# One GpSimd subtraction of 1536 columns instead of three of 512, in a kernel that splits its weights

## The chip, the cores and the metric

The kernel runs on one core of one Trainium2 chip. The metric is the device time of one execution in microseconds (us), the median of several runs. TensorE multiplies matrices, VectorE and GpSimd do element-wise work on SBUF (only VectorE also reads PSUM), ScalarE does activations and copies, and SyncE issues the loads.

## What is computed

One step of a decoder layer over 512 prompt rows and 8 sample rows, 520 tokens in all, with 1024 channels:

```
x <- LN1(alpha*x + 0.5*SwiGLU_1(x))          # first feed-forward part
z  = x @ w_in -> [C | B | h | p | g_a | g_p]
m  = sigmoid(g_a) * (B * conv3(C * h)) + sigmoid(g_p) * pooled(p)
x <- LN2(alpha*x + m @ w_out)
x <- LN3(alpha*x + 0.5*SwiGLU_2(x))          # second feed-forward part

SwiGLU(x) = (silu(x @ wg) * (x @ wu)) @ wd   # wg, wu: 1024 x 2816, wd: 2816 x 1024
```

All is in float32.

## The kernel before

Every operand of TensorE is split in two: a rounded part (hi) and what the rounding leaves, the rest (lo = value - hi). A product is then three passes: hi x hi, hi x lo and lo x hi. For a loaded weight, ScalarE makes hi by a copy to the rounded type, and GpSimd makes lo by a subtraction. TensorE waits for lo by a counter, `lo_ready`.

The tokens are two halves of 260 columns. The 2816 hidden channels of a feed-forward part are 22 columns f of 128. Columns 0 and 1 are made with plain products (the opening). For each of the columns 2 to 21 ("pairs": gate and up together) the kernel uses seven products of half size in place of eight, a Strassen-like scheme. It needs three loaded quarters of the weights, B11, B21 and B22, each 128 partitions x 512 columns, and four sums, T1 to T4. Of these, `weight_sums` (VectorE, L931, L936, L941) makes the sums, with the loaded B12 as one more input; ScalarE rounds; VectorE makes the rests of the sums in `rest_thirteen` (L945) and `rest_twenty_four` (L950); GpSimd makes the rests of B11, B21 and B22 in `split_pair` (L559). B11, B21 and B22 of a pair lie side by side in the three tensors raw, wh and wl.

The columns come in two stretches: 2 to 11, then eight down products; 12 to 21, then eight down products. All orders are written out by hand, one list of instructions for each engine.

TensorE, for pair f: P1 (weight B11), Q5 (T1), Q4 of the pair before (T4), P6 (T2), P2 (B21), Q3 (B22), P7 (T3). In the first pair of a stretch P2 comes right behind P1, and there is no Q4. Each product is 12 matmuls of 260 columns. P1, P2 and Q3 wait for `lo_ready`. Q5 and P7 use T1 and T3 from L945, P6 and Q4 use T2 and T4 from L950. Q4 of pair f also waits for `up_second` of pair f (VectorE, L998), which reads the bank that Q4 writes to.

VectorE, in the body of pair f: up_second(f-1) L998, gated_first(f-1) L1002, the weight sums of f+1 (L931, L936, L941), hid_pair(f-1) L1006 and L1011, rest_thirteen(f+1) L945, hid_rest(f-1) L982, rest_twenty_four(f+1) L950, for f from 3 to 10 the scaling of one tile of the residual (L1076), gate_first(f) L988, up_first(f) L993. L941 waits until the Q4 of two pairs earlier has used the place of T4.

ScalarE, in pair f: copies of three products out of PSUM, the rounding of the three loaded quarters of f+1 in one instruction of 1536 columns, sigmoids, and the roundings of the sums.

GpSimd, for each pair: it waits for the rounding (`hi_ready`) and for the last weight sum of the same pair (`t4_made`), then makes the three rests. Between the stretches, and in the other parts of the layer, it makes the rest of each chunk of weights in one instruction of up to 1536 columns (`split`, L550). It issues no loads.

SyncE loads each quarter as soon as the product that used its place two pairs earlier is done.

Of the kernel before, what the change touches and what calls it, by code (L numbers as in the profile page):

```python
# [30 lines left out]
ALU = mybir.AluOpType  # L31
ACT = mybir.ActivationFunctionType
AX_X = mybir.AxisListType.X
F32 = mybir.dt.float32
# [21 lines left out]
def build(nc, x_prompt, x_sample, state_conv, state_pool, ln1_g, ln1_b, ffn1_wg, ffn1_wu, ffn1_wd,  # L56
# [36 lines left out]
    with ExitStack() as ctx:  # L93
# [3 lines left out]
        def sem(name):  # L97
            return ctx.enter_context(nc.semaphore(name))
# [38 lines left out]
        wh_slot = wh[:].rearrange("p (s k) n -> p s (k n)", k=HK)  # L137
        wl_slot = wl[:].rearrange("p (s k) n -> p s (k n)", k=HK)
        raw_slot = raw[:].rearrange("p (s k) n -> p s (k n)", k=HK)
# [56 lines left out]
        def pair_tiles(ap, kk, h):  # L196

            return ap[:, 2 * kk:2 * kk + 2, h * H:(h + 1) * H]
# [24 lines left out]
        lo_ready = sem("lo_ready")  # L223
# [117 lines left out]
        area, slot, lands, free, landed, hi_no, lo_no = {}, {}, {}, {}, {}, {}, {}  # L341
        free_from = [0] * SLOTS
        landings = [0] * (SLOTS + 5)
        halves = [0, 0]

        def place(what, at, size, product, loaded=True):
            area[what], slot[what] = RING, at
            free[what] = max(free_from[at:at + size])
            free_from[at:at + size] = [number[product]] * size
            if loaded:  # L350
                landing(what, at)
# [21 lines left out]
        def set_of(f):  # L373
            return (f + 1) % 2

        def pair_place(n, f):
            for name, at in SET[set_of(f)].items():
                place((n, name, f), at, 1, (n, FOR[name], f), name[0] == "B")
            halves[0] += 1
            hi_no[n, f] = halves[0]  # L380
            for name in ("B11", "B21", "B22"):
                halves[1] += 1
                lo_no[n, name, f] = halves[1]

        for n in range(2):
            for j in range(4):
                open_place((n, "open", j), j, (FIRST, SECOND)[n], 0)
            for g, (f0, f1) in enumerate(SPANS):
                for f in range(f0, f1):
                    pair_place(n, f)  # L390
                for d in range(K):
                    chunk_place((n, "down", g, d), (8, 11, 0, 3)[d % 4], 3)
                    if (n, g) == (0, 1) and d in (3, 4, 5):
                        for j in {3: (0, 1), 4: (2,), 5: (3,)}[d]:
                            open_place(("mix", j), j, MIXED, number[0, "P7", KF - 1])
            if n == 0:
                for c in range(4, 12 * G):
                    chunk_place(("mix", c), 2 * ((c + 4) % 7), 2)
                for d in range(K - 1):
                    chunk_place(("out", d), 2 * ((12 * G + d + 4) % 7), 2)  # L400
                open_place(("out", K - 1), 0, LAST, number[0, "down", 1, K - 1])
# [6 lines left out]
        def held(part, what):  # L408
            return area[what][part][:, slot[what] * HK:slot[what] * HK + size_of(what), :]
# [15 lines left out]
        def pair_no(n, f):  # L425
            return (KF - 2) * n + f - 1
# [108 lines left out]
        @block.gpsimd  # L535
        def _(pool):
            made = Signal(const_ready)
            made.on(nc.gpsimd.memset(ident[:], 0.0))
            pool.wait_ge(const_ready, 1)
            made.on(nc.gpsimd.affine_select(out=ident[:], in_=ident[:], compare_op=ALU.not_equal, fill=1.0,  # L540
                                            base=0, pattern=[[-1, P]], channel_multiplier=1))
            made.on(nc.gpsimd.memset(ones_mean[:], 1.0 / D))
            assert made.n == 3
            for i in range(max(POOL_WINDOWS) - 1):
                made.on(nc.gpsimd.memset(rcount[:, i:i + 1], 1.0 / (i + 1)))

            def split(what):

                pool.wait_ge(hi_ready, hi_no[what])
                nc.gpsimd.tensor_tensor(held(LO, what), held(RAW, what), held(HI, what).bitcast(F32),  # L550
                                        ALU.subtract).then_inc(lo_ready, 1)

            def split_pair(n, f):
                pool.wait_ge(hi_ready, hi_no[n, f])

                pool.wait_ge(t4_made, pair_no(n, f))
                for name in ("B11", "B21", "B22"):
                    s = slot[n, name, f]
                    nc.gpsimd.tensor_tensor(wl_slot[:, s, :], raw_slot[:, s, :], wh_slot[:, s, :].bitcast(F32),  # L559
                                            ALU.subtract).then_inc(lo_ready, 1)  # L560

            def split_ffn(n, f_first):
                for g, (f0, f1) in enumerate(SPANS):
                    for f in range(f0 if g else f_first, f1):
                        split_pair(n, f)
                    for d in range(K):
                        split((n, "down", g, d))
                        if (n, g) == (0, 1) and d in (3, 4, 5):
                            for j in {3: (0, 1), 4: (2,), 5: (3,)}[d]:
                                split(("mix", j))  # L570

            def x_lo(n, h):

                for kk in range(K // 2):
                    pool.wait_ge(norm[n].round, 4 * h + kk + 1)
                    nc.gpsimd.tensor_tensor(pair_tiles(xl, kk, h), pair_tiles(x32, kk, h),
                                            pair_tiles(xh, kk, h).bitcast(F32), ALU.subtract).then_inc(norm[n].ready, 1)

            for j in range(4):
                split((0, "open", j))  # L580
            split_ffn(0, 2)
            for h in range(2):
                x_lo(0, h)

            nc.gpsimd.memset(pext[:, 0:16], 0.0).then_inc(pads_made, 1)
            nc.gpsimd.memset(uext[:, 0:2], 0.0).then_inc(pads_made, 1)
            for c in range(4, 12 * G):
                split(("mix", c))
            for d in range(K):
                split(("out", d))  # L590
            for j in range(4):
                split((1, "open", j))
            split_pair(1, 2)
            for h in range(2):
                x_lo(1, h)
            split_ffn(1, 3)

            pool.wait_ge(norm[2].offset, 2)
            for kk in range(1, K // 2):
                nc.gpsimd.tensor_tensor(pair_tiles(x32, kk, 1), pair_tiles(x32, kk, 1), offset_twice,  # L600
                                        ALU.subtract).then_inc(pool_minus, 1)
# [1131 lines left out]
```

## Time and profile before

| | before |
|---|---|
| median of 3 runs | 1096.61 us (1094.86 to 1097.17) |
| the profiled execution | 1095.99 us |
| its span, first to last instruction | 1094.2 us |
| TensorE matmul busy | 1059.0 us, 97% |
| VectorE busy | 709.8 us, 65% |
| ScalarE busy | 437.1 us, 40% |
| GpSimd busy | 510.5 us, 47% |
| mean granted TensorE clock | 0.993 |
| L559, the changed line | 120 instructions, 221.7 us |

Busy shares are means over parts of the kernel with different limits. In timelines each row has start and duration in us. An instruction that is shown as running may in part be held up by something that it shares with another engine; the record has no mark for that. Neighbouring records of one engine overlap by a little. In a merged row, xN stands for N instructions of a kind, one behind the other.

### The profile page before, as it was taken

What the parts mean: (1) busy time and instruction counts of PE and PEld (TensorE: products, weight loads), DVE (VectorE), ACT (ScalarE), POOL (GpSimd) and SP (SyncE); (2) the same over time, 40 slices, a digit from 0 to 9 for tenths busy, and PEclk for the clock granted to TensorE, in tenths of its full rate; (3) what the DMA queues carried; (4) which work ended last, traced back from release to release, by engine and by line L of the source; (5) the groups of instructions that cost most, each with busy time, mean ns of one, the idle gap of its engine ahead of it and who ended that gap; (6) DMA issues with size and microseconds to landing.
All of it is one profiled execution on the core that took longest, in us unless ns stands there. A gap on an engine that the chain in (4) does not pass through costs nothing.

```text
span 1094.2 us, 20812 instructions
## 1 busy us (share of the span) xinstructions
PE 1059.0 (97%) x8731; PEld 1050.6 (96%) x8731; DVE 709.8 (65%) x1019; ACT 437.1 (40%) x658; POOL 510.5 (47%) x259
## 2 busy tenths in 40 slices
PE   8999999999999987999999999989999999999996
PEld 7999999999999987999999999988999999999996
DVE  6999921288847866353636437989996116887476
ACT  4555532155553442232231323455554223555224
POOL 4355554154566345444453445334655433566321
PEclk9999999999999998999999999999999999999999
DMA  9133234233355042232332425103334323333402
GB/s 254 36 101 113 73 106 116 77 101 113 97 136 135 18 104 58 83 100 80 97 101 79 115 82 154 40 1 97 97 97 135 88 68 97 114 100 87 120 26 78
DMA packets 195001, 103.29 MB, mean 94 GB/s; under 512 B 4420, under 2 KB 193428, under 8 KB 194901
## 3 DMA queue, kind: packets, MB, share of 16 engines
q1 hardware_dynamic: 194827, 101.85, 32.7%
q8 instruction: 69, 1.13, 0.4%
q10 hardware_dynamic: 82, 0.12, 0.1%
q14 instruction: 23, 0.19, 0.1%
HBM read 99.74 MB, written 2.48 MB: 93 GB/s over the span
## 4 chain that ended last, share of the span: by engine, by line
PE 82%; DVE 11%; issue 3%; ACT 2%; DMA 1%; POOL 1%; SPq 0%; DVEq 0%; ACTq 0%; POOLq 0%
PE ps L1293 13%; PE ps L1295 13%; PE ps L1294 13%; PE ps L1313 13%; PE ps L1310 13%; PE ps L1311 13%; DVE x L1169 1%; DVE xl L915 1%; DVE x L1150 1%; DVE form_lo L966 1%; DMA mixed_raw<-in_w_in_dram 1%; DMA raw<-in_ffn_wd_dram 1%; ACT wh L605 1%; PE ps L1416 1%; PE ps L1356 1%
## 5 line engine op out<-in xcount | busy, mean ns | idle before, releaser
L550 POOL TENSOR_TENSOR wl<-raw,wh 128x1024 fp32r<-128x1024 f32 (+3 forms) x83 | 225.3, 2721 | 237.5 <-ACT wh L605 237.4
L559 POOL TENSOR_TENSOR wl<-raw,wh 128x512 fp32r<-128x512 f32 x120 | 221.7, 1875 | 227.9 <-DVE raw L941 182.6
L605 ACT ACTIVATE wh<-raw 128x1024 fp32r<-128x1024 f32 (+3 forms) x203 | 238.4, 1179 | 193.2 <-DMA raw<-in_ffn_wd_dram 102.8
L1293 PE MATMUL ps<-form_hi,wh 128*128 128x260 f32 x640 | 181.7, 284 | 3.5 <-ACT temps L605 3.5
L1295 PE MATMUL ps<-form_hi,wl 128*128 128x260 f32 x640 | 181.0, 283 | 0.0
L1294 PE MATMUL ps<-form_lo,wh 128*128 128x260 f32 x640 | 180.9, 283 | 0.0
L1310 PE MATMUL ps<-xh,wh 128*128 128x260 f32 x640 | 168.2, 284 | 5.7 <-DVE ymix L1243 5.7
L1311 PE MATMUL ps<-xl,wh 128*128 128x260 f32 x640 | 167.5, 283 | 0.0
L1310 PE MATMUL ps<-hid_hi,wh 128*128 128x260 f32 x544 | 141.9, 282 | 0.0
L1311 PE MATMUL ps<-hid_lo,wh 128*128 128x260 f32 x544 | 141.8, 282 | 0.0
L1293 PE MATMUL ps<-xh,wh 128*128 128x260 f32 x480 | 136.9, 285 | 2.8 <-DVE temps L973 1.5
L1294 PE MATMUL ps<-xl,wh 128*128 128x260 f32 x480 | 136.0, 283 | 0.0
L1295 PE MATMUL ps<-xh,wl 128*128 128x260 f32 x480 | 135.5, 282 | 0.0
L1313 PE MATMUL ps<-xh,wl 128*128 128x260 f32 x640 | 129.5, 284 | 0.0
L1310 PEld LDWEIGHTS ps<-xh,wh 128*128 128x128 f32 x640 | 121.8, 190 | 6.0 <-DVE ymix L1243 6.0
L1293 PEld LDWEIGHTS ps<-form_hi,wh 128*128 128x128 f32 x640 | 120.4, 188 | 4.6 <-issue 3.3
L1311 PEld LDWEIGHTS ps<-xl,wh 128*128 128x128 f32 x640 | 121.3, 190 | 0.0
L1295 PEld LDWEIGHTS ps<-form_hi,wl 128*128 128x128 f32 x640 | 120.6, 188 | 0.0
L1294 PEld LDWEIGHTS ps<-form_lo,wh 128*128 128x128 f32 x640 | 120.5, 188 | 0.0
L1313 PE MATMUL ps<-hid_hi,wl 128*128 128x260 f32 x544 | 109.5, 283 | 0.0
L1310 PEld LDWEIGHTS ps<-hid_hi,wh 128*128 128x128 f32 x544 | 102.5, 188 | 0.0
L1311 PEld LDWEIGHTS ps<-hid_lo,wh 128*128 128x128 f32 x544 | 102.4, 188 | 0.0
(221 smaller groups left out, 2214.4 us busy)
## 6 DMA issues: line engine op xcount, KB each, us to landing
raw<-in_ffn_wg_dram SPq DMA_DIRECT2D x80, 256.0 KB, 3.3
raw<-in_w_in_dram SPq DMA_DIRECT2D x40, 512.0 KB, 3.9
raw<-in_ffn_wd_dram SPq DMA_DIRECT2D x16, 768.0 KB, 5.9
b<-in_ffn_wu_dram SPq DMA_DIRECT2D x40, 256.0 KB, 3.4
raw<-in_ffn_wu_dram SPq DMA_DIRECT2D x40, 256.0 KB, 3.0
raw<-in_ffn_wd_dram SPq DMA_DIRECT2D x16, 640.0 KB, 5.4
raw<-in_w_out_dram SPq DMA_DIRECT2D x7, 512.0 KB, 3.9
xrow<-in_x_prompt_dram SPq DMA_DIRECT2D x4, 512.0 KB, 5.4
```

Of the source, the lines that this page charges most:

```text
L550: nc.gpsimd.tensor_tensor(held(LO, what), held(RAW, what), held(HI, what).bitcast(F32), ALU.subtract).then_inc(lo_ready, 1)
L559: nc.gpsimd.tensor_tensor(wl_slot[:, s, :], raw_slot[:, s, :], wh_slot[:, s, :].bitcast(F32), ALU.subtract).then_inc(lo_ready, 1)
L605: return nc.scalar.activation(out, in_, ACT.Copy)
L915: tt(xl[:, k, :], x32[:, k, :], xh[:, k, :].bitcast(F32), ALU.subtract).then_inc(x_ready, 1)
L966: tt(form_lo[:, i, :], form32[:, i, :], form_hi[:, i, :].bitcast(F32), ALU.subtract).then_inc(form_ready, 1)
L1150: tt(pair_tiles(x32, kk, h), pair_tiles(x32, kk, h), offset_twice, ALU.subtract).then_inc(s.minus, 1)
L1293: mm(out, hi, vh, start=start and n == 1, stop=False, skip_group_check=more)
L1294: mm(out, hi, vl, start=False, stop=False, skip_group_check=more)
L1295: ins = mm(out, lo, vh, start=False, stop=n == count, skip_group_check=more)
L1310: mm(bank(pair, h), hi, half(vh, h), start=start and n == 1, stop=False)
L1311: mm(bank(pair, h), hi, half(vl, h), start=False, stop=False)
L1313: ins = mm(bank(pair, h), lo, half(vh, h), start=False, stop=stop and n == count)
```

## The change

For each pair GpSimd issues one subtraction over the three quarters that lie side by side, in place of three. The counter `lo_ready` goes up by one for a pair instead of three, so P1, P2 and Q3 all wait for the same count.

```
@@ -378,8 +378,8 @@
             halves[0] += 1
             hi_no[n, f] = halves[0]
+            halves[1] += 1
             for name in ("B11", "B21", "B22"):
-                halves[1] += 1
                 lo_no[n, name, f] = halves[1]
@@ -554,10 +554,9 @@
                 pool.wait_ge(hi_ready, hi_no[n, f])

                 pool.wait_ge(t4_made, pair_no(n, f))
-                for name in ("B11", "B21", "B22"):
-                    s = slot[n, name, f]
-                    nc.gpsimd.tensor_tensor(wl_slot[:, s, :], raw_slot[:, s, :], wh_slot[:, s, :].bitcast(F32),
-                                            ALU.subtract).then_inc(lo_ready, 1)
+                s = slot[n, "B11", f]
+                nc.gpsimd.tensor_tensor(wl_slot[:, s:s + 3, :], raw_slot[:, s:s + 3, :],
+                                        wh_slot[:, s:s + 3, :].bitcast(F32), ALU.subtract).then_inc(lo_ready, 1)
```

## Rows read from the trace of the kernel before

**Rows 1.** The page, part 1: engine, busy us, share, instructions.

```profile
PE 1059.0 (97%) x8731; PEld 1050.6 (96%) x8731; DVE 709.8 (65%) x1019; ACT 437.1 (40%) x658; POOL 510.5 (47%) x259
```

**Rows 2.** GpSimd's groups by shape: busy us, mean ns | idle before, us.

```profile
L559 POOL TENSOR_TENSOR wl<-raw,wh 128x512 fp32r<-128x512 f32 x120 | 221.7, 1875 | 227.9 <-DVE raw L941 182.6 <-ACT wh L605 45.3
...
L550 POOL TENSOR_TENSOR wl<-raw,wh 128x1536 fp32r<-128x1536 f32 x16 | 55.9, 3505 | 54.0 <-ACT wh L605 53.9
```

**Rows 3.** Timeline of GpSimd, one steady pair: the first instruction alone, all three.

```profile
100.66 1.29 POOL L559 TENSOR_TENSOR wl<-raw,wh 128x512 fp32r<-128x512 f32 x1 [4.36 <-DVE raw L941]
...
100.66 5.76 POOL L559 TENSOR_TENSOR wl<-raw,wh 128x512 fp32r<-128x512 f32 x3 [4.36 <-DVE raw L941]
```

**Rows 4.** Timeline of VectorE beside it, and one L1076 with GpSimd idle.

```profile
99.83 0.69 DVE L941 TENSOR_TENSOR raw<-raw 128x512 f32<-128x512 f32 x1
...
101.57 1.47 DVE L945 TENSOR_TENSOR wl<-raw,wh 128x1024 fp32r<-128x1024 f32 x1
...
103.57 1.71 DVE L950 TENSOR_TENSOR wl<-raw,wh 128x1024 fp32r<-128x1024 f32 x1
105.19 1.52 DVE L1076 TENSOR_SCALAR x<-x 128x520 f32<-128x520 f32 x1
...
107.31 0.41 DVE L998 TENSOR_TENSOR temps<-temps,ps 128x260 f32<-128x260 f32 x1
...
107.97 1.22 DVE L931 TENSOR_TENSOR raw<-raw,b 128x1024 f32<-128x1024 f32 x1
...
109.95 0.69 DVE L941 TENSOR_TENSOR raw<-raw 128x512 f32<-128x512 f32 x1
...
126.76 0.42 DVE L1076 TENSOR_SCALAR x<-x 128x520 f32<-128x520 f32 x1
```

**Rows 5.** Timelines of GpSimd and VectorE beside a GpSimd instruction of 1280 columns.

```profile
343.38 2.95 POOL L550 TENSOR_TENSOR wl<-raw,wh 128x1280 fp32r<-128x1280 f32 x1
...
343.75 3.14 DVE L1105 TENSOR_TENSOR temps<-temps 128x520 f32<-128x520 f32 x1 [2.58 <-ACT temps L662]
```

**Rows 6.** Timeline of TensorE's weight loads: first load of a Q4.

```profile
67.29 0.19 PEld L1293 LDWEIGHTS ps<-xh,wh 128*128 128x128 f32 x1 [0.24 <-issue]
...
107.83 0.19 PEld L1293 LDWEIGHTS ps<-xh,wh 128*128 128x128 f32 x1
...
138.43 0.19 PEld L1293 LDWEIGHTS ps<-xh,wh 128*128 128x128 f32 x1
...
763.41 0.19 PEld L1293 LDWEIGHTS ps<-xh,wh 128*128 128x128 f32 x1 [0.25 <-issue]
...
834.25 0.19 PEld L1293 LDWEIGHTS ps<-xh,wh 128*128 128x128 f32 x1
```

**Rows 7.** Second stretch: VectorE at pair 12, first load of Q4 of pairs 12 and 20.

```profile
223.56 1.47 DVE L945 TENSOR_TENSOR wl<-raw,wh 128x1024 fp32r<-128x1024 f32 x1 [2.64 <-ACT wh L605]
224.96 2.30 DVE L950 TENSOR_TENSOR wl<-raw,wh 128x1024 fp32r<-128x1024 f32 x1
...
228.38 0.19 PEld L1293 LDWEIGHTS ps<-xh,wh 128*128 128x128 f32 x1
...
309.13 0.19 PEld L1293 LDWEIGHTS ps<-xh,wh 128*128 128x128 f32 x1
```

**Rows 8.** Timelines at the start of pair 3 of the first part.

```profile
51.85 2.12 POOL L559 TENSOR_TENSOR wl<-raw,wh 128x512 fp32r<-128x512 f32 x1 [9.86 <-DVE raw L941]
...
52.83 2.22 DVE L950 TENSOR_TENSOR wl<-raw,wh 128x1024 fp32r<-128x1024 f32 x1
...
54.02 0.19 PEld L1293 LDWEIGHTS ps<-xh,wh 128*128 128x128 f32 x1 [0.79 <-POOL wl L559]
```

**Rows 9.** Timeline of VectorE at pair 2 of the first part.

```profile
40.80 2.29 DVE L966 TENSOR_TENSOR form_lo<-form,form_hi 128x1040 fp32r<-128x1040 f32 x1
```

**Rows 10.** An idle of TensorE; a window behind it, with granted clock (0.57).

```profile
409.76 0.19 PEld L1293 LDWEIGHTS ps<-qh,wh 128*128 128x128 f32 x1 [3.32 <-issue]
...
410.00:414.00 4.00, 4.00 (x22) 4.00 (x22) 3.93 (x6) 3.86 (x6) 3.60 (x2) 0.57 0.06 17
```

## The prediction

> **What bounds the kernel now.** I read the page first. TensorE is busy for 97% of the span [rows 1], so a gain has to come out of the last 3%, and a loss comes from anything that makes TensorE wait. GpSimd is at 47% and is no bound by its own sum. Then I asked for GpSimd's groups by shape: the changed line L559 makes 120 instructions of 512 columns, and the kernel already has sixteen of 1536 columns, which take 3.5 us each [rows 2]. The question is therefore not what the merged instruction costs GpSimd, but who stands beside it. For that I put the timelines of GpSimd and VectorE side by side for one pair [rows 3, 4]. I call the twelve matmuls of a product by its name in the code; "pair f" is what the kernel's loop over f does.
>
> The reader is to see three things there. GpSimd's first instruction starts 0.83 us after VectorE's L941 (the last weight sum) and takes 1.29 us; the three together take 5.76 us, so the second and third take about 2.2 us each [rows 3]. VectorE's L945 takes 1.47 us and ends 1.09 us after GpSimd's first one; L950 takes 1.71 us; L1076 takes 1.52 us although the same instruction takes 0.42 us when GpSimd is idle [rows 4]. Each of these VectorE instructions ends a fixed time after a GpSimd instruction ends, and each GpSimd instruction that met a VectorE one took 1 us longer. So the two engines take turns, one whole instruction at a time. Third, VectorE has no idle time between L941 at 99.83 and the next L941 at 109.95: its own work and its turns fill the 10.12 us. TensorE's Q4 starts 0.52 us after L998 starts (107.83 against 107.31) [rows 4, 6], because Q4 waits for up_second, which is L998. VectorE's length of turn thus sets the time of a pair in the pairs with a residual scaling (L1076); one Q4 in each feed-forward part even shows the wait as idle [rows 6].
>
> **Is a turn as long as the instruction?** Where GpSimd ran 1280 columns (2.95 us from 343.38), VectorE's L1105, issued at 343.75, took 3.14 us and ended 0.56 us after it, though it adds just 520 columns, half of L931's 1024 in 1.22 us [rows 4] [rows 5]. So the hold grows with the instruction, up to 1280 columns at least. The Trainium skill says the same (SBUF — State Buffer, Who interferes with whom): a VectorE instruction with two SBUF inputs and a GpSimd instruction that reads SBUF exclude each other for the whole instruction, and whichever issues first keeps the other out. By that rule this change speaks against itself, since it turns three short holds into one long one; the trace agrees up to 1280 columns and can't show 1536. The sum by the rule is the sum below.
>
> **The change in one pair.** Removed: two GpSimd instructions and two of three semaphore counts. Nothing moves in any queue, no DMA is touched. P1, Q3 and P2 all wait now for the end of the one instruction.
>
> GpSimd: starts at L941 + 0.83 as before, runs 3.51 us undisturbed [rows 2], ends at L941 + 4.34 (104.17 in the pair shown) instead of + 6.59. P1, which had waited for the first third only, begins two products before Q4. A product takes 10.09 / 7 = 1.44 us (a pair of the second stretch, below, has seven), so P1 begins near 104.95, at L941 + 5.12, and still finds its weight ready with 0.8 us to spare. That wait costs nothing in a steady pair.
>
> VectorE: L945 can't begin until the whole instruction is over: it ends at L941 + 5.43 instead of + 3.21, that is 2.22 us later. L950 no longer meets GpSimd and takes what L931 takes, which has its shape and kind and no company: 1.22 instead of 1.71, 0.49 back [rows 4]. That makes +1.73. Where L1076 follows, it takes 0.42 instead of 1.52: 1.10 back, which leaves +0.63. So a VectorE cycle becomes 10.12 + 0.63 = 10.75 us with the scaling. Without it, the cycle was 10.12 - 1.44 = 8.68 us (L1076's 1.52 less the 0.08 by which neighbouring records overlap) and becomes 8.68 + 1.73 = 10.41.
>
> **The sum over the kernel.** There are two feed-forward parts with 20 pairs each, in a first and a second stretch.
>
> First stretch: from Q4 of pair 3 to Q4 of pair 10, seven intervals, all with scaling. They took 71.14 us and 70.84 us (67.29 to 138.43, 763.41 to 834.25) [rows 6]. They become 7 x 10.75 = 75.25. Cost 4.11 + 4.41 = 8.52 us.
>
> Second stretch: TensorE sets the pace today, (309.13 - 228.38) / 8 = 10.09 us an interval [rows 7]. VectorE's 10.41 now exceeds it: eight intervals cost 8 x 0.32 = 2.54 us (with 10.093). The way in adds more. L945 at 223.56 ends 2.22 us later, at 227.25, and L950, which took 2.30 us, takes 1.22 after it and ends at 228.38 instead of 227.26. Q4 follows at 228.38, 1.12 us behind L950's old end, and 1.12 us is also what lies between L1076's end and Q4 in the pair of rows 4 and 6: it hangs on this chain and moves by 1.12. Together 3.66, twice: 7.32 us.
>
> Entry to pair 3: here VectorE's L945 had the first turn and GpSimd's first instruction took 2.12 us, from 51.85 to 53.97; TensorE already waited for it, 0.79 us, and starts P1 at 54.02 [rows 8]. L945 ended where L950's record begins, near 52.84, so the first third needed 1.13 us once it had its turn, 0.15 less than without company. Merged, it ends at 52.84 + 3.51 - 0.15 = 56.20. P1 is 2.22 us later, and the pairs behind it hang on it (VectorE's L950 is later by the same). The second part repeats this pattern. Cost 4.44 us.
>
> Pair 2 of the first part: L945 ends 2.2 us later and the L966 that took 2.29 us (a twin without company takes about 1.24) no longer waits [rows 9]: 1.16 us later, on the way to pair 3. In the second part pair 2's rests fall into the layer norm, among short VectorE instructions that also take turns; between nothing and the 1.16 of its twin I take 0.6. Pair 12's rests are made 10 us early beside a nearly idle VectorE, under TensorE's down product: nothing; without that cover they would cost what pair 3's do, 2.2.
>
> Terms: 8.52 + 7.32 + 4.44 + 1.16 + 0.6 = 22.0 us.
>
> The clock: TensorE's idle before P1 of pair 3 grows from 0.79 to 3.0 us. The nearest row is an idle of 3.32 us before 409.76, behind which the granted clock is 0.57 over 4 us [rows 10], part of it at the lower of the two levels, worth 4 x 0.43 = 1.7 us. Two such places: between 0 and 3.4 us; my idle is a little shorter than that row's, so I take half, 1.7.
>
> A last weighing: the Trainium skill (GPSIMD Engine Reference, section 3.1) gives 4497 ns for a two-input fp32 instruction of 2048 columns. As an estimate by that page, 1536 columns would take 3.37 us, 0.13 less than the row, and the loss would be about 4 us smaller over some 32 pairs. The kernel's own row of 1536 columns decides, 3.51.
>
> Sum: 22.0 + 1.7 = 23.7. Profiled execution 1095.99 us (span 1094.2 and 1.8 around it) + 23.7 = 1119.7. The median of the runs is 0.62 above that execution, so I forecast 1120.3 us, 2.2% slower.
>
> **Rivals.**
> (a) The second stretch hides its part. VectorE has 10.09 - 8.68 = 1.41 us free there and the cost is 1.73; if the true cost is under 1.41, the eight intervals cost nothing, and perhaps half of the entry's 1.13 goes too. For: 0.32 is a small difference of two sums. Against: each term repeats to 0.02 us. Time about 1120.3 - 6.2 = 1114.
> (b) The long instruction is worked off in pieces between which VectorE gets its turns. Then L945 is no later than today, but GpSimd ends at L941 + 6.6 and P1 (needed at + 5.2) waits for it. From P1 to the end of Q4 it is three products, 4.3 us, and the next L941 needs the place that Q4 frees: a cycle of at least 6.6 + 4.3 + some 0.3 for two handovers = 11.2 us in 30 intervals, 1.1 more each, 1096.6 + 33 = 1130. Against: the 1280 columns [rows 5].
> (c) Not slower. The two engines would have to run side by side without taking turns for the length of this instruction. It decides at GpSimd's end: if the instruction ends within 4.3 us of its start while L945 still gets through at its old time, the steady pairs lose nothing, and L950 and L1076 gain up to 1.6 us of turns. TensorE could then give back only the 0.03 us a pair between 10.12 and 10.09, and pair 3's waits: 1094 to 1097. For: GpSimd's total drops from 5.76 to 3.5 us. Against: no VectorE instruction with two SBUF inputs in rows 4, 5 or 8 passed a GpSimd one.
> (d) More than I see: the lower clock in both places and longer, or ScalarE's copies falling behind in the shifted order. 1124 to 1130.
>
> **How the numbers follow.** Forecast 0.78, (a) 0.07, (b) 0.04, (c) 0.04, (d) 0.07. Within the forecast the clock term moves by 1.7 either way and the steady costs by 0.1 us in 30 intervals (7 and 8, twice), 3 us. The range 1112 to 1125 holds the forecast case, (a), and part of (d). A change under 0.2%, 2.2 us, can't be told from none. Slower 0.95, same 0.03, faster 0.02.
>
> **What the changed profile would show.** L559 x40 at about 3.5 us, 140 us in all. L945 takes about 3.7 us (issued at L941 + 1.74, ended at + 5.43), L950 1.2, L1076 0.42. L941 repeats every 10.75 us in the first stretch and every 10.41 in the second, with no VectorE idle in either. TensorE idles before Q4 in each pair, 0.3 to 0.7 us, and about 3.0 us before P1 of pair 3. The prediction is wrong if L945's time stays near 1.5 (then b or c), if Q4 follows Q4 every 10.09 us in the second stretch (a), or if the norm and mix stages grow too, where I put nothing.

## The result, and the profile after

The changed kernel takes 1129.89 us (median of 4 runs, 1127.39 to 1132.2) against 1096.22 us for the kernel before (4 runs too): a ratio of 1.0306, 95% interval 1.0292 to 1.0319. It is slower, as forecast, but by 33.7 us where I had 24, and outside the range (1112 to 1125). The profiled execution has a span of 1128.3 us, 34.1 more than before.

All later listings name lines of the changed kernel: from `split_pair` on they are one lower than before (L559 is L558, L941 is L940, L945 is L944, L982 is L981, L950 is L949, L998 is L997).

The page, part 1, and the groups of GpSimd, VectorE and, last, of TensorE's matmuls that P1 begins with, answering to [rows 1, 2]:

```profile
PE 1069.0 (95%) x8731; PEld 1055.2 (94%) x8731; DVE 757.6 (67%) x1019; ACT 436.0 (39%) x658; POOL 431.3 (38%) x179
...
L558 POOL TENSOR_TENSOR wl<-raw,wh 128x1536 fp32r<-128x1536 f32 x40 | 142.9, 3574 | 324.7 <-DVE raw L940 292.1 <-ACT wh L604 32.6
...
L944 DVE TENSOR_TENSOR wl<-raw,wh 128x1024 fp32r<-128x1024 f32 x40 | 136.5, 3412 | 5.3 <-ACT wh L604 5.3
L949 DVE TENSOR_TENSOR wl<-raw,wh 128x1024 fp32r<-128x1024 f32 x40 | 55.8, 1396 | 0.0
...
L1292 PE MATMUL ps<-xh,wh 128*128 128x260 f32 x480 | 138.9, 289 | 25.6 <-DVE hid_lo L981 18.5
```

GpSimd has lost 79 us of busy time and TensorE's share has fallen to 95%. L944 takes 3.4 us on the mean, 1.9 more than L945 did. The hold is there, and it lasts as long as the instruction. In the last row, 18.5 us of TensorE's idle end with L981, which is hid_rest; the kernel before has 2.8 us of idle in this group, and none by hid_rest.

The timelines of one steady pair of the first stretch, VectorE, then GpSimd, then TensorE's weight loads at P1 and Q4. They answer to [rows 3, 4] and the Q4 of [rows 6]:

```profile
83.21 0.69 DVE L940 TENSOR_TENSOR raw<-raw 128x512 f32<-128x512 f32 x1 [0.16 <-PE ps L1294]
...
84.95 3.69 DVE L944 TENSOR_TENSOR wl<-raw,wh 128x1024 fp32r<-128x1024 f32 x1
88.56 0.68 DVE L981 TENSOR_TENSOR hid_lo<-ps,hid_hi 128x520 fp32r<-128x520 f32 x1
89.17 1.21 DVE L949 TENSOR_TENSOR wl<-raw,wh 128x1024 fp32r<-128x1024 f32 x1
90.31 0.42 DVE L1075 TENSOR_SCALAR x<-x 128x520 f32<-128x520 f32 x1
...
91.32 0.41 DVE L997 TENSOR_TENSOR temps<-temps,ps 128x260 f32<-128x260 f32 x1
...
94.09 0.69 DVE L940 TENSOR_TENSOR raw<-raw 128x512 f32<-128x512 f32 x1 [0.16 <-PE ps L1294]
...
84.04 3.52 POOL L558 TENSOR_TENSOR wl<-raw,wh 128x1536 fp32r<-128x1536 f32 x1 [7.36 <-DVE raw L940]
...
89.36 0.19 PEld L1292 LDWEIGHTS ps<-xh,wh 128*128 128x128 f32 x1 [0.73 <-issue]
...
92.24 0.19 PEld L1292 LDWEIGHTS ps<-xh,wh 128*128 128x128 f32 x1
```

Every VectorE time of the prediction is met: L944 3.69 us ending at L940 + 5.43, L949 1.21, L1075 0.42, GpSimd ending at + 4.35. But the cycle is 10.88 us, not 10.75, and TensorE's idle stands in front of P1 (89.36), not in front of Q4. GpSimd had ended at 87.56, 1.8 us before P1. What ends 0.12 us before P1 is L981, hid_rest: 88.56 + 0.68 = 89.24. P1 writes to the bank that hid_rest of two pairs earlier reads, and so it waits for `hid_ready`, besides `lo_ready`. From P1 the chain goes on through two products to Q4 (2.88 us), and L940 waits for Q4's end: it starts 1.85 us after Q4 starts, with an idle of 0.16 that the profile puts down to TensorE. 6.15 + 2.88 + 1.85 = 10.88.

In the second stretch VectorE has no scaling to do, and yet the cycle is the same; only its idle before L940 grows:

```profile
977.41 0.69 DVE L940 TENSOR_TENSOR raw<-raw 128x512 f32<-128x512 f32 x1 [0.50 <-PE ps L1294]
...
982.76 0.69 DVE L981 TENSOR_TENSOR hid_lo<-ps,hid_hi 128x520 fp32r<-128x520 f32 x1
...
988.29 0.69 DVE L940 TENSOR_TENSOR raw<-raw 128x512 f32<-128x512 f32 x1 [0.51 <-PE ps L1294]
...
983.56 0.19 PEld L1292 LDWEIGHTS ps<-xh,wh 128*128 128x128 f32 x1 [0.73 <-issue]
```

Again 10.88 us from L940 to L940, and P1 0.11 us behind the end of L981. In 32 of the 40 pairs, all but the first two of each stretch, P1 starts 0.12 us behind the end of L981. The kernel before, in the pair of [rows 4] and two pairs later: L982, which is hid_rest there, and P1.

```profile
102.96 0.69 DVE L982 TENSOR_TENSOR hid_lo<-ps,hid_hi 128x520 fp32r<-128x520 f32 x1
...
104.92 0.19 PEld L1293 LDWEIGHTS ps<-xh,wh 128*128 128x128 f32 x1
...
124.52 0.69 DVE L982 TENSOR_TENSOR hid_lo<-ps,hid_hi 128x520 fp32r<-128x520 f32 x1
...
125.33 0.19 PEld L1293 LDWEIGHTS ps<-xh,wh 128*128 128x128 f32 x1
```

In the first of them hid_rest ended at 103.65, 1.3 us ahead of P1. In the second, where L945 had taken 2.27 us, it ended at 125.21 and P1 followed by 0.12 us: the wait could be seen in one pair of the kernel before.

Where the 34.1 us of the span came in, read by laying the start times of the same VectorE instructions of both traces side by side (us; the first event is 0.6 early). The sums are named by the pair that they are for; the mix part is the middle of the layer, between the two feed-forward parts:

```
part of the kernel                               forecast   measured
pairs 2 and 3, first feed-forward part              3.4        2.8
second layer norm (rests of pair 2)                 0.6        2.1
pair 3, second part                                 2.2        1.6
first stretches, from pair 4's sums to their end    8.5       11.9
second stretches                                    7.3       16.1
clock, by forecast at pair 3; seen in the mix part  1.7        2.2
start and end of the kernel                         0         -2.6
```

### The profile page after: what moved, and what is told of

Same layout as the page of the kernel before. It is cut to its first block and busy times, and to the rows that moved or that the text cites. A ratio compares the mean times of both kernels' runs of the same rounds, so it can differ in the third digit from the quotient of the medians.

```text
span 1128.3 us, 20732 instructions
## 1 busy us (share of the span) xinstructions
PE 1069.0 (95%) x8731; PEld 1055.2 (94%) x8731; DVE 757.6 (67%) x1019; ACT 436.0 (39%) x658; POOL 431.3 (38%) x179
## 5 line engine op out<-in xcount | busy, mean ns | idle before, releaser
L558 POOL TENSOR_TENSOR wl<-raw,wh 128x1536 fp32r<-128x1536 f32 x40 | 142.9, 3574 | 324.7 <-DVE raw L940 292.1
L1292 PE MATMUL ps<-xh,wh 128*128 128x260 f32 x480 | 138.9, 289 | 25.6 <-DVE hid_lo L981 18.5
L944 DVE TENSOR_TENSOR wl<-raw,wh 128x1024 fp32r<-128x1024 f32 x40 | 136.5, 3412 | 5.3 <-ACT wh L604 5.3
L1309 PEld LDWEIGHTS ps<-xh,wh 128*128 128x128 f32 x640 | 122.5, 191 | 6.0 <-DVE ymix L1242 6.0
L1292 PEld LDWEIGHTS ps<-xh,wh 128*128 128x128 f32 x480 | 90.3, 188 | 32.7 <-issue 26.6
```

The costliest lines, as they stand in the source:

```text
L558: nc.gpsimd.tensor_tensor(wl_slot[:, s:s + 3, :], raw_slot[:, s:s + 3, :], wh_slot[:, s:s + 3, :].bitcast(F32), ALU.subtract).then_inc(lo_ ...
L944: tt(thirteen(wl_slot, n, f), thirteen(raw_slot, n, f), thirteen(wh_slot, n, f).bitcast(F32), ALU.subtract).then_inc(t13_ready, 1)
L1292: mm(out, hi, vh, start=start and n == 1, stop=False, skip_group_check=more)
L1309: mm(bank(pair, h), hi, half(vh, h), start=start and n == 1, stop=False)
```

## The experiments

Each ran beside the kernel before on the same chip; before stood at 1095.86 us with the first four, 1096.15 with the next four and 1095.37 with the last. After the result I held theory A: P1 waits for hid_rest, which is queued behind the held rest_thirteen. B was that P1 waits for GpSimd's end because of the one count, C that VectorE is full, as predicted.

**e1, hid_rest ahead of rest_thirteen, in the changed kernel.**

```
                        if f > f0:
                            hid_pair(f - 1)
+                       if f > f0:
+                           hid_rest(f - 1, (f - 1) % 2)
                        if f + 1 < f1:
                            rest_thirteen(n, f + 1)
-                       if f > f0:
-                           hid_rest(f - 1, (f - 1) % 2)
```

> The changed kernel with one move: VectorE makes hid_rest (the rest of the hidden tile, 0.69 us) before rest_thirteen instead of behind it. Theory A (P1 waits for hid_rest, which sits behind the rest_thirteen that the 1536-column instruction holds up; P1 starts 6.15 us after the last weight sum): the wait goes, hid_rest ends about 3.2 us after the last weight sum, and the pair falls from 10.88 to about 10.1 us in both stretches; 7 x 0.74 x 2 + 8 x 0.79 x 2 = 23 us less, near 1107 us. Theory B (P1 waits for GpSimd's end, the one count): nothing changes, 1130 us. Theory C (VectorE is simply full, as predicted): the move saves at most the 0.6 us that ScalarE's copy overlaps, and no idle of TensorE before P1 was there to save; 1120 to 1125 us.

Measured: 1106.6 us, ratio 1.0095 (1.0059 to 1.0132). VectorE in a pair of the first stretch:

```profile
102.07 0.69 DVE L940 TENSOR_TENSOR raw<-raw 128x512 f32<-128x512 f32 x1
...
104.58 0.70 DVE L981 TENSOR_TENSOR hid_lo<-ps,hid_hi 128x520 fp32r<-128x520 f32 x1 [0.67 <-ACT hid_hi L604]
105.19 2.31 DVE L944 TENSOR_TENSOR wl<-raw,wh 128x1024 fp32r<-128x1024 f32 x1
107.42 1.21 DVE L949 TENSOR_TENSOR wl<-raw,wh 128x1024 fp32r<-128x1024 f32 x1
```

hid_rest is over at 3.2 us after L940, L944 spends in the hold only what hid_rest, with its wait of 0.67 us for ScalarE's rounding, has left of it (2.31 us instead of 3.69), and the cycle is 10.14 us in the first stretch and 10.09 in the second. 23 us of the 33.7 are gone with one reordering, while GpSimd's instruction is as long as ever (3.51 us). B falls: the count and GpSimd's end are where they were. C allows a far smaller saving than 23 us, but it too would have VectorE's cycle near 10.1 us after the move, so the number against it is that of e8. The move is not free at the entries: from pair 3's sums to pair 4's it takes 11.39 and 12.60 us here, against 9.93 and 9.89 in the changed kernel, each time with a lower granted clock.

**e2, B11 alone, then B21 and B22 in one instruction of 1024 columns.** The added line, here and in e4, e5, e7 and e9, says which quarters share one instruction and one count.

```
+            return [("B11",), ("B21", "B22")]
```

> The kernel before with two instructions per pair: B11 alone (512 columns), then B21 and B22 together (1024). Theory A: rest_thirteen is held by the 512 columns only, so it and hid_rest end where they did before; the 1024 columns are in front of rest_twenty_four, which no P1 waits for. VectorE's cycle is 10.13 us with the scaling and 9.8 without: 1096 to 1099 us. Theory B (fewer counts cost): P1 has its own count here, also 1097. A loss in proportion to what is merged (long holds as such) would give 1110 us or more.

Measured: 1103.04 us, ratio 1.0068 (1.0044 to 1.0093). That is 4 us above the range expected. The steady cycles are as forecast, 10.13 and 10.09. But in the profiled execution two pairs of the second stretch have 11.03 us. There ScalarE's rounding had waited for a load:

```profile
238.33 1.49 ACT L609 ACTIVATE wh<-raw 128x1536 fp32r<-128x1536 f32 x1 [0.42 <-DMA raw<-in_ffn_wg_dram]
...
239.89 3.65 POOL L563 TENSOR_TENSOR wl<-raw,wh 128x512 fp32r<-128x512 f32 x2 [5.18 <-ACT wh L609]
...
241.27 3.36 DVE L949 TENSOR_TENSOR wl<-raw,wh 128x1024 fp32r<-128x1024 f32 x1
```

The two GpSimd instructions run from 239.89 to 243.54 without a break. The weight rest of VectorE (here L949) came at 241.27, just too late to go between them, and had to stand out the whole long one, which delayed hid_rest too. These two pairs are 1.9 us. Beside them the trace has 2.2 us for the two ways into the second stretches, and 3.6 us more between the sums of pairs 2 and 3 of the second part, with two windows of lower clock, and it begins 1.7 us earlier. So a long hold is safe only while its partner keeps arriving first.

**e3, three instructions of 512, one count behind the third.**

```
+                for name in ("B11", "B21", "B22"):
...
+                                                  ALU.subtract)
+                ins.then_inc(lo_ready, 1)
```

> The kernel before with its three instructions of 512 columns, but with the count only behind the third, so that P1 waits for all three as in the changed kernel. Theory A: holds are as before, hid_rest is early, but P1 now finds GpSimd's end at 6.65 us after the last weight sum; the pair is 6.65 + 2.88 + 1.85 = 11.4 us, 30 intervals x 1.3 plus two entries of 3.5 us: 1138 to 1144 us. If the count costs nothing and the length of the instruction is all: 1097 us.

Measured: 1152.6 us, ratio 1.0526 (1.0485 to 1.0568); the cycle is 11.34 us in both stretches. P1's idle is now GpSimd's by name:

```profile
91.48 0.19 PEld L1294 LDWEIGHTS ps<-xh,wh 128*128 128x128 f32 x1 [1.19 <-POOL wl L559]
```

The cycle came as worked out, the total 9 us above the range. From the weight sums of pair 3 to those of pair 4 it takes 12.67 us against 8.28 before, twice, 1.8 us more than expected in all; from pair 13's to pair 14's 14.45 and 14.41 against 10.27, where a steady pair's 1.3 more was expected, 5.7 us more in all; and the stretch around the second layer norm is 1.5 us longer. The mean granted clock is 0.982 against 0.993. The change is thus two things that partly cancel. Waiting for all three alone costs 57 us; that they are one shorter instruction takes this wait away again and puts the smaller one at hid_rest in its place.

**e4, merged only in pairs 13 to 21.**

```
+            return [("B11", "B21", "B22")] if f > 12 else [("B11",), ("B21",), ("B22",)]
```

> One instruction of 1536 columns only for the pairs 13 to 21 of each feed-forward part, three of 512 elsewhere. Theory A: the pair is 10.88 us there instead of 10.09, 16 intervals x 0.79 = 12.6 plus the two ways in, 1.1 each: 1111 to 1113 us. The prediction's term for the second stretch (VectorE full at 10.41) says 7.3 us: 1104 us. If the second stretch hides it, 1099.

Measured: 1110.59 us, ratio 1.0138 (1.0103 to 1.0173), just under the range of theory A; cycles 10.88 in the second stretch, 10.12 in the first. This is the term that I had at 7.3 us; it is 14.7, with an interval of 11 to 19.

**e5, B11 and B21 in one instruction, then B22 alone.** The groups of e2 the other way round.

> The kernel before with B11 and B21 in one instruction of 1024 columns, then B22 alone. Theory A (P1 hangs on hid_rest behind the held rest_thirteen, and the cycle is the larger of P1's start + 4.73 us, VectorE's own work and TensorE's 10.09): the hold ends 3.2 us after the last weight sum, hid_rest ends at 4.9, P1 starts at 5.0: 9.8 by that way, so it does not show; VectorE's own cycle is about 10.17 with the scaling. 1098 to 1102 us, with 1.1 us at each entry to pair 3. If a cost grew evenly with the columns merged, 1024 of 1536 would bring some two thirds of the extra columns' loss: 1113 us.

Measured: 1100.99 us, ratio 1.005 (1.0026 to 1.0073); cycles 10.13 and 10.09. The loss is not in proportion to the columns merged: at 1024 columns in front of hid_rest the steady pairs lose nothing. The 4.8 us that are left (5.1 in the trace) lie elsewhere: 4.3 between the sums of pairs 2 and 3 of the second part, with a lower granted clock, 2.2 at the ways into the second stretches, 1.1 behind pair 3's sums, with a start that is 1.8 earlier.

**e6, the reordering of e1 in the kernel before.**

> Control for the moved hid_rest: the kernel before, three instructions of 512, with hid_rest ahead of rest_thirteen. If the move were a gain by itself, this would be faster than the kernel before. Theory A: hid_rest was in time there, so nothing is gained; rest_thirteen now meets GpSimd's second instruction and VectorE's cycle with the scaling becomes about 10.27: 1097 to 1099 us.

Measured: 1097.1 us, ratio 1.0011 (0.9992 to 1.0029), cycles 10.28 (10.12 before) and 10.09. The time can't be told from that of the kernel before. The reordering helps only where there is a long hold to come out of.

**e7, merged only in pairs 2 and 3.**

```
+            return [("B11", "B21", "B22")] if f < 4 else [("B11",), ("B21",), ("B22",)]
```

> One instruction of 1536 columns for pairs 2 and 3 of each feed-forward part only. What the steady pairs cost is left out; what stays are the entries to pair 3 and the rests in the second layer norm, where TensorE and the norm wait at once: 2.8 + 2.1 + 1.6 us as read from the changed profile, so 1101 to 1104 us. With the steady pairs of theory A alone (22 us of the 33.7) it would be 1096, and the missing part would lie elsewhere.

Measured: 1103.18 us, ratio 1.0085 (1.0051 to 1.0118), 7.0 us. No steady pair is touched here, so this is the entries' and the layer norm's own part (interval 5.6 to 12.9). Its trace has 4.3 us at the entries, as the changed kernel has, and 3.8 in the layer norm, where the changed kernel has 2.1.

**e8, 1280 columns, then 256; P1 waits for the first.**

```
+                for k0, k1 in ((0, 10), (10, 12)):      # blocks of 128 columns
+                    nc.gpsimd.tensor_tensor(wl[:, at + k0:at + k1, :], raw[:, at + k0:at + k1, :],
```

> The three rests in two instructions of 1280 and 256 columns; P1 waits for the first. The hold is 0.57 us shorter than with 1536. Theory A: P1 starts at 6.15 - 0.57 = 5.58 us after the last weight sum, the cycle is 5.58 + 4.73 = 10.31 in both stretches; with entries of about 1.7 us each 1106 to 1110 us. The recorded theory (VectorE full) says 10.18 with the scaling and TensorE's 10.09 without: no loss at all in the second stretch.

Measured: 1111.29 us, ratio 1.0149 (1.012 to 1.0177). This was the run that sets A and C against each other by a number, with the hold 0.57 us shorter. The end of hid_rest, the last weight sum behind it, and P1:

```profile
96.39 0.69 DVE L984 TENSOR_TENSOR hid_lo<-ps,hid_hi 128x520 fp32r<-128x520 f32 x1
...
101.92 0.69 DVE L943 TENSOR_TENSOR raw<-raw 128x512 f32<-128x512 f32 x1 [0.17 <-PE ps L1297]
...
97.19 0.19 PEld L1295 LDWEIGHTS ps<-xh,wh 128*128 128x128 f32 x1 [0.18 <-POOL wl L560]
```

P1 follows hid_rest's end (97.08) by 0.11 us, and the cycle is 10.33 us in both stretches: A said 10.31, C 10.18 and 10.09. The total is 1.3 us above the range that A gave. The profile names GpSimd as releaser of the idle before P1, but its first instruction, the one that P1 waits for, was over before hid_rest began, since L947 had its turn between the two. The second, which ends at 97.06, has no part in it by the code, though the times alone could not tell it from hid_rest; e1 does. P1 waits for two counters, and the label is not always the one that it waited for.

**e9, what the account says can be mended.** One instruction of 1536 columns in 17 of the 20 pairs, three of 512 in pairs 2, 3 and 13, and hid_rest first.

```
+            return [("B11",), ("B21",), ("B22",)] if f in (2, 3, 13) else [("B11", "B21", "B22")]
```

> One instruction of 1536 columns in 17 of the 20 pairs of each feed-forward part, three of 512 in pairs 2, 3 and 13, and hid_rest ahead of rest_thirteen. If the steady wait (undone by the move) and the entries (undone by the three pairs) are all that the change costs, nothing is left: cycles of 10.14 and 10.09 us, 1096 to 1098 us, the same as the kernel before within 0.2%. If a merged instruction has a further cost of its own, 34 of 40 of it is still here and the time stays above 1100 us.

Measured: 1096.86 us, ratio 1.0006 (0.999 to 1.0022). One of the twelve executions took 2916.74 us; the ratio leaves it out, and its cause is not known. Nothing is left of the loss, though 34 of 40 merged instructions stay. Nothing is gained over the kernel before either.

## Why the prediction was right and wrong, point by point

- **The whole instruction holds VectorE out**: right, now at 1536 columns. L944 took 3.69 us; all VectorE terms of the pair came within 0.02 us. Piecewise turns (b) and running side by side (c) did not occur. The Trainium skill (SBUF — State Buffer, Who interferes with whom) says that the one that issues first has the shared port for the whole instruction and the other is blocked; this trace agrees, with these 3.69 us.
- **"It still finds its weight ready with 0.8 us to spare. That wait costs nothing in a steady pair."** This is the step that failed. The sentence is true of `lo_ready`, but P1 has a second wait in the same place of the code, `hid_ready`, and I never asked who brings it. It is hid_rest, the next instruction behind L945 in VectorE's order. I had moved L945's end by 2.22 us, and carried the delay along VectorE's list to L998 and Q4, but not into what the instructions passed on the way release. hid_rest had 1.3 us to spare; 2.22 was too much. TensorE then idles 0.73 us before P1 and the cycle is 10.88 us in both stretches, where the sum had 10.75 and 10.41 and the idle before Q4. The way from a late P1 over Q4 to the next L940 stood in rival (b), at 11.2 us, and e3 shows it, at 11.34; what was missing is the counter that makes P1 late. e1 and e8 show that it is this one.
- **First stretches, 8.5 us**: 10.3 from pair 4's sums to pair 11's, by the cycle of 10.88 instead of 10.75, and 1.5 more on the way out of the stretch.
- **Second stretches, 7.3 us**: 16.1. The ways in cost 1.1 each, as forecast (11.38 us from pair 13's sums to pair 14's, against 10.27). But here VectorE's own cycle, 10.41 by forecast, was nearly hidden behind TensorE's 10.09, so the missed wait, at 10.88, more than doubled the term. This is most of the error. e4 measured it by itself.
- **Rival (a)**, the second stretch hides its part: wrong, and for the same reason.
- **Entry to pair 3**: P1 waited for GpSimd as forecast. The last weight sum of pair 4 came 1.7 us later by it in the first part and 1.6 in the second; I had 2.2. TensorE's idle before this P1 was 1.53 us in the first part, part of the wait being taken up by the lower clock, and 2.96 in the second, for a forecast of 3.0. Pair 2 of the first part cost 1.1 for a forecast of 1.16.
- **Layer norm 2, 0.6 us**: 2.1. The hold brought 0.6 up to the statistics; the rest came with a lower granted clock, 0.72 in the window from 716 to 722 us, where the kernel before had 1.00 between 701 and 706. e4 bears this out: its instructions between the sums of pairs 2 and 3 are those of the kernel before, and it too is 1.5 us longer there, with a mean clock of 0.97 (rows below). e7, with the instructions of the changed kernel there, has 0.95 and is 3.8 us longer. So the 0.6 for the hold fits these traces, and the rest is the clock, which I had not expected here; why it falls is open.
- **The clock, 1.7 us**: the size was near, the place wrong. TensorE's clock did fall, but in pair 2, behind an idle of 2.70 us, while the next P1 waited for GpSimd anyway (1.53 us, row below), so that it cost nothing there. Elsewhere it cost: in the mix part two windows of 4 us show 0.50 and 0.66 in a row, where the kernel before had one at 0.58 and then 1.00. And behind the idle of 2.96 us in the second part, for which I had counted half of such a loss, the clock stayed at 1.00. That the size came out near is luck.

P1 of pair 3 in the first and the second part, and windows of the changed kernel (us, busy of five engines, then granted clock):

```profile
56.72 0.19 PEld L1292 LDWEIGHTS ps<-xh,wh 128*128 128x128 f32 x1 [1.53 <-POOL wl L558]
...
772.70 0.19 PEld L1292 LDWEIGHTS ps<-xh,wh 128*128 128x128 f32 x1 [2.96 <-POOL wl L558]
...
440.00:444.00 4.00, 3.51 (x16) 3.51 (x17) 1.14 (x2) 0.00 (x0) 0.00 (x0) 0.50 0.00 0
444.00:448.00 4.00, 4.00 (x25) 4.00 (x25) 0.00 (x0) 0.00 (x0) 0.00 (x0) 0.66 0.00 0
716.00:722.00 6.00, 6.00 (x41) 6.00 (x40) 3.21 (x11) 1.01 (x3) 0.00 (x0) 0.72 0.30 87
...
772.00:776.00 4.00, 3.29 (x27) 3.30 (x28) 4.00 (x6) 0.84 (x3) 0.65 (x1) 1.00 0.05 11
```

From the last sum of pair 2 to that of pair 3, second part: the kernel before, the changed kernel, e4 and e7.

```profile
687.58:747.10 59.52, 53.65 (x452) 52.18 (x451) 53.29 (x85) 29.25 (x53) 17.26 (x11) 1.00 0.10 28
...
705.93:767.53 61.60, 55.18 (x451) 53.72 (x451) 53.81 (x85) 29.25 (x53) 16.55 (x9) 0.97 0.09 27
...
693.84:754.89 61.05, 55.20 (x451) 53.74 (x451) 53.29 (x85) 29.25 (x53) 17.25 (x11) 0.97 0.09 27
...
688.77:752.09 63.32, 56.70 (x451) 55.23 (x451) 53.39 (x85) 29.25 (x53) 16.81 (x9) 0.95 0.09 26
```

The parts add up: e4 (14.7) and e7 (7.0) give 21.7; with the steady first stretches, 10.3, and their way out, 1.5, both read in the changed kernel's trace, that is 33.5 against the measured 33.7. That it fits so well is in part luck: e4 and e7 have intervals several us wide, and both hold time of a lower clock around the second layer norm. What stays open is why the clock fell in just these windows of the mix part, where the work is unchanged, and in the layer norm. No run was made for it.

## What to carry to other kernels

When an instruction is held up, list every wait that the instructions behind it on its engine release, not only the wait that the change is about; and for the engine that sets the pace list every counter that each step waits for, with who brings it and how early. Fewer and larger instructions on one engine are no saving if another engine takes turns with it: the busy time of GpSimd fell by 79 us and the kernel lost 34. The loss in the steady pairs has a threshold, here between 1024 (e5) and 1280 columns (e8) in front of hid_rest, and the short job that others wait for should stand ahead of the long one that may be held.

## What the runs showed of the hardware

The turns between VectorE and GpSimd are whole instructions also at 1536 columns: VectorE's 1024-column subtraction, issued 0.91 us after GpSimd's start, ended 1.08 us after GpSimd's end and took 3.69 us in all. With the same instructions the outcome depends on who arrives first: 1.47 us for rest_thirteen in most pairs of e2, and 3.36 in the pair where a load was late. The granted clock can differ between kernels where the work is the same: from pair 2's sums to pair 3's in the second part the kernel before took 59.52 us at a mean of 1.00, and e4, with the same instructions there, 61.05 us at 0.97. Such windows move a total by some 2 us, which is 0.2%.
